# Routed tokens gathered and returned in the rounded float format, as a rounded part and a remainder

## The reference: what is computed

```python
def moe_ffn(xn, router_w, router_b, w1, w3, w2):
    logits = (xn @ router_w).astype(jnp.float32) + router_b.astype(jnp.float32)
    top_v, top_i = lax.top_k(logits, TOP_K)
    w = jax.nn.softmax(top_v, axis=-1)
    gate = jnp.sum(jax.nn.one_hot(top_i, N_EXPERTS, dtype=jnp.float32) * w[..., None], axis=-2)
    out = jnp.zeros_like(xn)
    for e in range(N_EXPERTS):
        out = out + gate[..., e:e + 1] * swiglu(xn, w1[e], w3[e], w2[e])
    return out
```

## Time and profile before

| | |
|---|---|
| median of 3 runs | 2017.08 us (2014.29 to 2018.54) |
| profiled execution, first to last instruction (span) | 2015.0 us |
| its own time, timer included | not listed apart; the runs shown lie from 0.7 below the span to 3.5 above |
| PE busy | 1861.7 us, 92% |
| DVE busy | 1504.8 us, 75% |
| ACT busy | 1191.6 us, 59% |
| part with the eight jobs, from the first gather to the last | 931.9 to 1942 us |
| granted TensorE clock, mean | 0.962 |

### The profile page before, as it was taken

One profiled execution on the slowest core, in us unless ns is written; L12 is line 12 of the kernel. 1 busy time (PEld: TensorE's weight loads), 2 busy tenths in 40 slices (PEclk: granted clock), 3 DMA queues, 4 the chain that ended last, 5 costly groups with the idle time before them and its releaser, 6 DMA issues.

```text
span 2015.0 us, 29746 instructions
## 1 busy us (share of the span) xinstructions
PE 1861.7 (92%) x10906; PEld 1627.8 (81%) x10907; DVE 1504.8 (75%) x1893; ACT 1191.6 (59%) x1601; POOL 337.7 (17%) x151
## 2 busy tenths in 40 slices
PE   5979778999987989697999999999999999999977
PEld 4868778999986868696888888888888888888866
DVE  7495875555554685955988889888898888988954
ACT  3547523343333548324777777777787777877742
POOL 4634840000005635640000000000000000000000
PEclk8999988999988989897999999999999999999989
DMA  7323433454532422442898988989899898998950
GB/s 276 126 95 127 167 110 126 184 194 158 219 117 93 161 100 92 162 152 84 340 381 311 383 337 347 375 313 373 340 355 374 313 375 332 362 372 308 379 205 22
DMA packets 36789, 485.40 MB, mean 241 GB/s; under 512 B 4048, under 2 KB 6368, under 8 KB 7136
## 3 DMA queue, kind: packets, MB, share of 16 engines
q1 hardware_dynamic: 34272, 481.93, 62.5%
q10 hardware_dynamic: 2432, 2.31, 0.4%
HBM read 483.15 MB, written 1.07 MB: 240 GB/s over the span
## 4 chain that ended last, share of the span: by engine, by line
PE 75%; DVE 16%; issue 4%; ACT 4%; DMA 1%; DVEq 0%; ACTq 0%; SPq 0%
PE work L854 16%; PE work L856 16%; PE work L855 16%; PE acc L856 6%; PE acc L855 6%; PE acc L854 6%; PE work L1056 2%; ACT w_hi L752 2%; DVE x L1273 1%; PE misc L862 1%; PE pv_ps L1105 1%; DVE spare L1358 1%; DVE spare L1370 1%; DVE spare L1372 1%; DVE spare L1367 1%
## 5 line engine op out<-in xcount | busy, mean ns | idle before, releaser
L1596 DVE TENSOR_TENSOR w_lo<-raw,w_hi 128x1024 fp32r<-128x1024 f32 x672 | 775.8, 1220 | 70.5 <-ACT w_hi L752 69.5
L752 ACT ACTIVATE w_hi<-raw 128x1024 fp32r<-128x1024 f32 x672 | 667.5, 1055 | 96.0 <-DMA raw<-in_moe_w 46.8
L441 POOL TENSOR_TENSOR w_lo<-raw,w_hi 128x1024 fp32r<-128x1024 f32 x136 | 335.3, 2482 | 558.4 <-ACT w_hi L436 558.2
L854 PE MATMUL work<-w_hi,bias_r 128*128 128x512 f32 x896 | 356.8, 398 | 4.3 <-DVE w_lo L1596 4.3
L856 PE MATMUL work<-w_hi,bias_r 128*128 128x512 f32 x896 | 350.7, 391 | 0.0
L855 PE MATMUL work<-w_lo,bias_r 128*128 128x512 f32 x896 | 350.1, 391 | 0.0
L854 PE MATMUL work<-x_r,w_hi 128*128 128x256 f32 x1088 | 323.6, 297 | 17.4 <-DVE x_r L1210 16.5
L436 ACT ACTIVATE w_hi<-raw 128x1024 fp32r<-128x1024 f32 x236 | 242.7, 1051 | 160.2 <-PE work L856 111.8
L855 PE MATMUL work<-x_r,w_hi 128*128 128x256 f32 x1088 | 313.1, 288 | 0.0
L856 PE MATMUL work<-x_r,w_lo 128*128 128x256 f32 x1088 | 312.9, 288 | 0.0
L854 PEld LDWEIGHTS work<-x_r,w_hi 128*128 128x128 f32 x1088 | 213.9, 197 | 29.1 <-issue 20.1
(11 more groups left out here) (271 smaller groups left out, 2587.0 us busy)
## 6 DMA issues: line engine op xcount, KB each, us to landing
raw<-in_moe_w SPq DMA_DIRECT2D x168, 2048.0 KB, 9.6
raw<-in_mix_w SPq DMA_DIRECT2D x34, 2048.0 KB, 8.0
raw<-in_dense_w SPq DMA_DIRECT2D x21, 2048.0 KB, 8.1
raw<-in_ple_w SPq DMA_DIRECT2D x4, 2048.0 KB, 10.5
areaK<-in_ple_p SPq DMA_DIRECT2D x2, 1024.0 KB, 5.5
hT<-in_xT SPq DMA_DIRECT2D x1, 1024.0 KB, 5.9
gate_a<-bias_line ACTq DMA_DIRECT2D x1, 1024.0 KB, 5.9
areaB<-bias_line ACTq DMA_DIRECT2D x1, 1024.0 KB, 8.5
```

The lines of the kernel that those rows point to most:

```text
L441: eng.tensor_tensor(unit(w_lo, g), raw_part(g), unit(w_hi, g).bitcast(F32), ALU.subtract).then_inc(split_ok, 1)
L752: act.activation(w_hi[u][:, :], raw[n % RING][:, (i % 4) * QUARTER:(i % 4 + 1) * QUARTER], ACT.Copy).then_inc(hi_ok, 1)
L854: pe.matmul(out, stat[0], move[0], start=start, stop=False, skip_group_check=True)
L1596: dve.tensor_tensor(w_lo[u][:, :], raw[n % RING][:, (i % 4) * QUARTER:(i % 4 + 1) * QUARTER], w_hi[u][:, :].bitcast(F32), ALU.subtract).th ...
```

## The change

The token matrix that is gathered from is stored as a rounded part (`areaA_r`, ACT as before) and a remainder (`areaB_r`, four new DVE subtractions while the experts are chosen). `m_pick` is written rounded, and is exact there. The gather has two rounded matmuls for each float32 one: 32 in place of 16, with 128 moving columns.

The result of an expert is multiplied by the gate weight of its slot as ACT takes it from PSUM (`scale=slot_gate`, rounded part `y_hi`), and the matrix that returns it to its tokens is a 0/1 matrix `m_pickT`. The remainder `y_lo` is made by a new DVE instruction of 128 x 1024 that reads PSUM again; another of 128 x 256 makes `m_pickT`. Both are in `split_y`, called in DVE's `job` at i = 3. TensorE waits for it instead of for ACT, and has 16 rounded matmuls of 256 columns where it had 8 in float32. The gate weight of a slot is the sum along its row of the turned slot matrix, which ACT accumulates as it copies that matrix out. The semaphores of skipped jobs are carried along.

```diff
@@ -203,7 +203,7 @@
         areaB, areaB_r = shared("areaB", KT * T)
         areaK = sb("areaK", [P, KT * T])
         gate_a_flat, gate_a_r = shared("gate_a", KT * T)
-        gate_b_flat = sb("gate_b", [P, KT * T])
+        gate_b_flat, gate_b_r = shared("gate_b", KT * T)
         spare, spare_r = shared("spare", CHUNK)
         bias_flat, bias_r = shared("bias", HEADS * BAND)
         lru = sb("lru", [P, KT, CONV - 1 + T])
@@ -328,17 +328,21 @@
         out_done = sem("out_done")
 
 
-        xn_tok = q_tok
+        xn_tok = areaA_r[:, :].rearrange("p (t n) -> p t n", t=TT)
+        xn_tok_lo = areaB_r[:, :].rearrange("p (t n) -> p t n", t=TT)
         xg_hi = bias_r[:, 0:1024].rearrange("p (k n) -> p k n", k=KT)
         xg_lo = bias_r[:, 1024:2048].rearrange("p (k n) -> p k n", k=KT)
         hidT_hi = bias_r[:, 2048:2560].rearrange("p (f n) -> p f n", f=FT)
         hidT_lo = bias_r[:, 2560:3072].rearrange("p (f n) -> p f n", f=FT)
-        y_sb = spare[:, 0:D]
+        y_hi = spare_r[:, 0:D]
+        y_lo = spare_r[:, D:2 * D]
         scr = lru[:, :, :].rearrange("p k t -> p (k t)")
         m_silu = scr[:, 0:512]
         m_hid = scr[:, 512:1024]
         gbf = gate_b_flat
-        m_pick = gbf[:, 0:256].rearrange("p (t n) -> p t n", t=TT)
+        m_pick = gate_b_r[:, 0:256].rearrange("p (t n) -> p t n", t=TT)
+        m_pickT = gate_b_r[:, 512:768]
+        slot_gate = gbf[:, 768:769]
         m_gpick = gbf[:, 256:512].rearrange("p (t n) -> p t n", t=TT)
         m_gpickT = gbf[:, 1024:1280]
         iota_f = gbf[:, 1536:1664]
...
@@ -738,7 +744,7 @@
             def take_y(j):
 
                 act.wait_ge(part_used, j * JOB_Q + UNITS_HELD)
-                act.activation(y_sb, acc[0][:, :], ACT.Copy).then_inc(m_y, 1)
+                act.activation(y_hi, acc[0][:, :], ACT.Copy, scale=slot_gate).then_inc(m_yhi, 1)
 
             def job(j, first):
 
@@ -769,7 +775,7 @@
                         take_y(j + first)
                     if i == M_GT + AHEAD - 1:
                         act.wait_ge(m_gturned, j + (first + 1))
-                        act.activation(m_gpickT, misc[:, 0:T], ACT.Copy).then_inc(m_gtaken, 1)
+                        act.activation(m_gpickT, misc[:, 0:T], ACT.Copy, accum_out=slot_gate).then_inc(m_gtaken, 1)
                     for c in range(FC):
                         if i == M_W1[c] + AHEAD:
                             silu(c)
...
@@ -1053,23 +1059,25 @@
                     for kk in range(4):
                         k = 4 * half + kk
                         for tt in range(TT):
-                            mm = pe.matmul(work[half][:, kk * P:(kk + 1) * P], xn_tok[:, tt, k * P:(k + 1) * P],
-                                           m_pick[:, tt, :], start=(tt == 0), stop=(tt == TT - 1))
+                            pe.matmul(work[half][:, kk * P:(kk + 1) * P], xn_tok[:, tt, k * P:(k + 1) * P],
+                                      m_pick[:, tt, :], start=(tt == 0), stop=False)
+                            mm = pe.matmul(work[half][:, kk * P:(kk + 1) * P], xn_tok_lo[:, tt, k * P:(k + 1) * P],
+                                           m_pick[:, tt, :], start=False, stop=(tt == TT - 1))
                     mm.then_inc(m_gathered, 1)
 
             def combine(n):
 
 
                 pe.wait_ge(m_y, n + 1)
-                pe.wait_ge(m_gtaken, n + 1)
                 for q in range(4):
                     if q >= 2:
 
                         pe.wait_ge(m_added, n * 4 + (q - 1))
                     for kk in range(2):
                         k = 2 * q + kk
-                        mm = pe.matmul((pv_ps, misc)[q % 2][:, T * kk:T * kk + T], y_sb[:, k * P:(k + 1) * P],
-                                       m_gpickT, start=True, stop=True)
+                        out = (pv_ps, misc)[q % 2][:, T * kk:T * kk + T]
+                        pe.matmul(out, y_hi[:, k * P:(k + 1) * P], m_pickT, start=True, stop=False)
+                        mm = pe.matmul(out, y_lo[:, k * P:(k + 1) * P], m_pickT, start=False, stop=True)
                     mm.then_inc(m_combined, 1)
 
             def job(j, first):
@@ -1167,7 +1175,7 @@
                 pe.matmul(misc[:, 72:80], before, mk[:, 1, :], start=False, stop=True)
                 pe.matmul(misc[:, 80:88], ones[:, :], mk[:, 0, :], start=True, stop=False)
                 pe.matmul(misc[:, 80:88], ones[:, :], mk[:, 1, :], start=False, stop=True).then_inc(ranked, 1)
-                pe.wait_ge(tok_ok, 4)
+                pe.wait_ge(tok_lo, 4)
 
                 wait_full(pe, l, "out", KT - 1)
                 pe.sem_inc(part_used, UNITS_HELD)
@@ -1489,6 +1497,12 @@
                 step.settle()
                 dve.sem_inc(route_masks, 1)
                 dve.tensor_tensor(df, m2, m1, ALU.subtract).then_inc(route_diff, 1)
+                for i in range(4):
+                    dve.wait_ge(tok_ok, i + 1)
+                    tt, half = divmod(i, 2)
+                    cols_ = slice(half * 512, (half + 1) * 512)
+                    dve.tensor_tensor(xn_tok_lo[:, tt, cols_], quad[i], xn_tok[:, tt, cols_].bitcast(F32),
+                                      ALU.subtract).then_inc(tok_lo, 1)
                 dve.wait_ge(route_exp, 1)
                 step(dve.tensor_scalar(w2, ex, 1.0, None, ALU.add))
                 step.settle()
@@ -1579,6 +1593,14 @@
                     dve.tensor_tensor(xg_lo[:, k, :], work[half][:, :].rearrange("p (k n) -> p k n", k=4),
                                       xg_hi[:, k, :].bitcast(F32), ALU.subtract).then_inc(m_xg, 1)
 
+            def split_y(n):
+
+                dve.wait_ge(m_yhi, n + 1)
+                dve.wait_ge(m_gtaken, n + 1)
+                dve.tensor_scalar(m_pickT, m_gpickT, 0.0, None, ALU.is_gt)
+                dve.scalar_tensor_tensor(out=y_lo, in0=acc[0][:, :], scalar=slot_gate, in1=y_hi.bitcast(F32),
+                                         op0=ALU.mult, op1=ALU.subtract).then_inc(m_y, 1)
+
             def add_combined(n):
 
                 for q in range(4):
@@ -1598,6 +1620,8 @@
 
                 for i in range(JOB_Q):
                     lo_m(i)
+                    if i == AHEAD - 1:
+                        split_y(j + first)
                     if i == 3 + AHEAD:
                         add_combined(j + first)
                     if i == M_W3[1]:
@@ -1622,6 +1646,7 @@
                 dve.sem_inc(m_xg, 2)
                 dve.sem_inc(m_hid_ok, FC)
                 dve.sem_inc(m_hidT, FC)
+                dve.sem_inc(m_y, 1)
                 dve.sem_inc(m_added, 4)
                 dve.sem_inc(m_built, 1)
 
...
@@ -1646,6 +1672,7 @@
                         job(r, EXPERTS)
                 lo.n = phase_q[(l, "ple")]
                 lo.to(phase_q[(l, "ple")] + 2)
+                split_y(JOBS)
                 add_combined(JOBS)
 
             lo = Line(dve, split_lo)
```

More of the change, by code:

```diff
@@ L385, in trunk @@
         m_y = sem("m_y")
+        m_yhi = sem("m_yhi")
+        tok_lo = sem("tok_lo")
         m_gturned = sem("m_gturned")
@@ L787, in skipped @@
                 act.sem_inc(m_hidT_hi, FC)
-                act.sem_inc(m_y, 1)
+                act.sem_inc(m_yhi, 1)
                 act.sem_inc(m_gtaken, 1)
@@ L1631, in moe @@
                 step(dve.memset(m_gpickT, 0.0))
+                step(dve.memset(slot_gate, 0.0))
                 step.settle()
```

## The result

The changed kernel takes 2023.98 us (median of 5 runs, 2023.06 to 2027.71), the kernel before 2017.08 (median of 5 runs, 2014.29 to 2018.54): a ratio of 1.0043, 95% interval 1.0032 to 1.0054. It is slower by 6.9 us. The forecast was 2033, its range 2016 to 2046, and slower with a chance of 0.75. The sign and the mechanism at the heads of the jobs hold; the change is less than half of the +15.7 us that were forecast.

The account below looks back on a forecast made before the run. TensorE, busy 92%, was taken to bound the kernel, with VectorE's first sum ending level at the heads. Heads 4.8, last return 0.7, clock 8.8 and 1.4 make +15.7 us on the median 2017.1: 2032.8, range 2016 to 2046.

Parts of the forecast that it names:

- The gather brings nothing: Gather on TensorE: 32 rounded matmuls at 0.11 us take 3.5 us, against 3.49 before, no gain.
- The return's gain turns into a wait for VectorE's first sum: Return at each job's head: 1.5 us gained on TensorE becomes a 2.65 us pause; +0.6 a head, 4.8 in all.
- The last return: Return after the last job: VectorE's split after two weight quarters delays its start and last sum, +0.7 us.
- While experts are chosen: Four new VectorE subtractions (4 x 0.60 us) fit in 2.68 us of idle time; nothing counted.
- The clock at the heads: Pauses inside the return bring half-clock stretches, 1.6 us each, after 5.5 of 8 pauses: +8.8 us.
- The clock at the end: After the last return TensorE may stay at half clock for the norm's 16 matmuls: 3.4 us with 0.4, +1.4 us.

Follow-up runs that it names:

- the part alone: The changed kernel with its gather undone (float32, 16 matmuls), so only the return is in the rounded format: 2024.20 us, ratio 1.0045.
- gather-only kernel: The kernel before with the rounded gather alone (token remainder, 32 rounded matmuls), the return still float32: 2015.48 us, ratio 1.000.

## Why the prediction was right, and where it was off

- **The gather brings nothing.** Right. Predicted 0.11 a matmul and 3.5 us; measured 0.11 and 3.60. The row of weight loads for matmuls of 8 columns gave the price. It was taken at half clock, 0.217, so the 0.109 that the prediction says it shows at full clock was half of it, an estimate; the 0.11 at full clock and the 0.21 of the first gather at half clock bear it out. The run with 64 columns rules the columns out. The Trainium skill's 81 ns for 128 columns ("TensorE: Matmul & The Clock Gate", "Back-to-back issue gap") is not what this kernel shows: 112 ns.
- **The return's gain turns into a wait for VectorE's first sum.** Right, and shown by experiment from three sides: less VectorE work ahead of the sum (job -1.0 us), the sum earlier (job -2.0), and the part alone (the whole loss). Predicted +0.6 a head and a pause of 2.65 us; measured +0.5 at seven heads and 2.49 us, counted in the same way (1075.89 to 1078.38). The new VectorE instructions were 1.40 us, not 1.5. The first head was taken to be like the others and is not: its return became 0.4 us shorter. That makes 3.1 us for the eight, where the sum has 4.8.
- **The last return.** The sum of the stretch is +1.4 where I had 0.7. The start moved by 5.5 us, not 5.2, of which 0.2 are ScalarE's copy, which itself began that much later behind the gather; and from the start to the last sum are 4.1 us, not 3.7.
- **While experts are chosen.** Right: the four subtractions lie in the idle time; that wait is now 0.28 us.
- **The clock at the heads: the step that failed in size.** "I take 5.5 of the 8 pauses: 8.8 us." One of eight pauses was followed by a stretch at half clock in the changed kernel's profile, two of eight in the return-only kernel, with 1.2 to 1.6 us each: 1.2 to 3 us for 8.8. The price of one was about right; how often it comes was read off four pauses elsewhere in the program, and four are few. What makes the heads different is not shown. With one stretch in place of 5.5 the forecast's own sum is 4.8 + 0.7 + 1.2 + 1.4 = 8.1, against 6.9 measured. That they lie so close is luck in part: in the profile the heads came out lower (3.1), and the last return and the end higher.
- **The clock at the end: foreseen in kind, too small.** The sum has 1.4 us; from the last sum to the end the profile has +3.7. It is not one profile's accident. In the six other traces that have a rounded return, 7 to 10 of the norm's 16 matmuls began at half clock, and from the norm's start to the end are 50.7 to 51.5 us (51.7 in the changed kernel); in the three with the float32 return none did, and it is 48.0 to 48.8. With the float32 return 7.1 to 9.6 us lie between the last return's start and the norm's, and the clock rose within them; with the rounded return they are 5.5 us, and the clock rose only during the norm. So much of what the shorter return saves there is lost in the norm.
- **Not foreseen:** the first gather's 6.64 us in place of 5.04 (first start to last). All four profiles with the rounded gather of 128 columns have 6.64 or 6.65 us there, all at half clock; those with float32 have 5.0 in two and 6.3 to 6.4 in three. No median shows it, and the +2.0 us of the table up to the second gather is in part the luck of the profile before: the kernel before with the early sums needs 129.64 us from the first to the second gather, the gather-only kernel 129.68, the changed kernel 129.40 and the kernel before 127.43. The first gather in the kernel before (two stretches) and in the changed one:

```profile
931.90:935.00 3.10, 3.07 (x14) 0.50 0.02 5
935.10:937.00 1.90, 1.90 (x19) 1.00 0.00 0
931.00:937.60 6.60, 6.60 (x32) 0.50 0.01 2
```

## What to carry to other kernels

Making one engine's step cheaper pays only if what it hands over to comes along: look for the wait that already ends within 0.1 us of the step, and count every instruction that the change puts ahead of it on the other engine. Where a loop written out by position decides that, look at the position too: here one number (7 to 5) turned 7 us lost into 9 us gained, of which 4 come with the old format as well. And a matmul that loads new weights each time had a floor here, 0.11 us in this format at full clock: halving its columns from 128 to 64 brought nothing.

## What the runs showed of the hardware

A stretch at half clock can follow narrow rounded matmuls although TensorE issues without a pause. In the kernel with 64 columns six of the eight gathers behind the first had such a stretch begin in their last 1.2 us or within a microsecond behind them; in the changed kernel none had. Two of them, each with the gather ahead of it (stretch, TensorE busy, granted clock, DMA share, GB/s):

```profile
1182.20:1185.20 3.00, 3.00 (x30) 1.00 1.04 399
1185.40:1192.00 6.60, 6.60 (x19) 0.50 0.73 293
1311.00:1314.20 3.20, 3.20 (x31) 1.00 1.09 394
1315.00:1318.30 3.30, 3.30 (x9) 0.50 0.94 392
```

Its gathers have half the columns of the changed kernel's. Five of the stretches lie in the seven jobs between gathers, and these five jobs are 0.8 to 2.3 us longer, 7 us together; its one run is 9 us over the changed kernel's median. The first gather differs between the formats too: in all five profiles with float32 the clock rose to full during it, in all five with rounded matmuls it stayed at half throughout. Why is not shown, and the kernel with 64 columns ran only once.
